# First tile of the input projection from the unnormed input, and the memory's keys and values beside the input's norm

## What is computed

```python
def rms_norm(x, g, eps=EPS):
    return x * lax.rsqrt(jnp.mean(x * x, axis=-1, keepdims=True) + eps) * g

def reference(x, mem, ...):
    mkv = (rms_norm(mem, mem_norm_g) @ mem_w_kv).reshape(B, M, 2, MEM_HEADS, MEM_HEAD_DIM)
    mem_k = rms_norm(mkv[:, :, 0], mem_k_g)
    mem_v = mkv[:, :, 1]
    for l in range(DEPTH):
        h = rms_norm(x, norm_mix_g[l])
        proj = h @ w_in[l]
        ...
```

## Time and profile before

| | us |
|---|---|
| median of 3 runs | 2043.94 |
| lowest, highest | 2038.11, 2048.75 |
| profiled execution | 2036.31 |
| its span, first to last instruction | 2034.5 |
| TensorE matmuls, busy | 1954.1 (96% of the span) |
| VectorE busy | 637.1 |
| ScalarE busy | 385.8 |
| GpSimd busy | 74.4 |
| granted TensorE clock, mean | 0.994 |

### The profile page before, as it was taken

One profiled execution on the slowest core, in us unless ns is written; L12 is line 12 of the kernel. 1 busy time (PEld: TensorE's weight loads), 2 busy tenths in 40 slices (PEclk: granted clock), 3 DMA queues, 4 the chain that ended last, 5 costly groups with the idle time before them and its releaser, 6 DMA issues. The chain is left out here.

```text
span 2034.5 us, 27414 instructions
## 1 busy us (share of the span) xinstructions
PE 1954.1 (96%) x11538; PEld 1049.1 (52%) x11538; DVE 637.1 (31%) x1297; ACT 385.8 (19%) x739; POOL 74.4 (4%) x138
## 2 busy tenths in 40 slices
PE   8999999999999999999799999989999999999996
PEld 5445995455544444443254489754554444444443
DVE  4244665224311111111144556551452111111112
ACT  3221325224000000000122222350520000000001
POOL 3000000000000000000200010010000000000001
PEclk9999999999999999999999999999999999999998
DMA  8000001521699999999850000032239999999996
GB/s 351 1 1 0 3 3 50 207 83 42 261 410 426 427 427 429 428 429 427 333 214 1 0 2 3 10 139 110 83 124 393 423 428 427 429 429 428 427 428 237
DMA packets 51548, 481.88 MB, mean 237 GB/s; under 512 B 7216, under 2 KB 12080, under 8 KB 23792
## 3 DMA queue, kind: packets, MB, share of 16 engines
q1 hardware_dynamic: 49136, 471.91, 55.7%
q0 software_dynamic: 2304, 8.39, 1.1%
HBM read 461.14 MB, written 19.14 MB: 236 GB/s over the span
## 5 line engine op out<-in xcount | busy, mean ns | idle before, releaser
L1898 PE MATMUL bank<-ring,hT 128*64 128x512 f32 x2080 | 471.3, 596 | 14.0 <-DVE hT L1928 8.3
L1898 PEld LDWEIGHTS bank<-ring,hT 128*64 128x64 f32 x2080 | 143.2, 137 | 286.9 <-issue 264.2
L842 PE MATMUL bank<-hT,ring 128*128 128x512 f32 (+1 forms) x608 | 263.3, 594 | 1.8 <-DVE hT L289 1.0
L1891 PE MATMUL bank<-arena 128*128 128x256 f32 x1088 | 252.0, 386 | 3.8 <-DVE arena L1918 3.8
L1891 PEld LDWEIGHTS bank<-arena 128*128 128x128 f32 x1088 | 201.9, 190 | 78.9 <-issue 50.3
L1905 PE MATMUL bank<-ring,arena 128*64 128x512 f32 x1040 | 236.7, 597 | 5.5 <-DMA ring<-in_we 4.5
L842 PEld LDWEIGHTS bank<-hT,ring 128*128 128x128 f32 (+1 forms) x608 | 114.3, 189 | 148.0 <-issue 146.9
L1928 DVE TENSOR_TENSOR hT<-bank,colp 128x512 f32<-128x512 f32 x68 | 47.0, 692 | 399.6 <-PE bank L1891 399.6
L2188 ACT ACTIVATE arena<-bank 128x256 f32<-128x256 f32 x65 | 24.9, 383 | 662.3 <-PE bank L1877 662.3
L1905 PEld LDWEIGHTS bank<-ring,arena 128*64 128x64 f32 x1040 | 70.6, 137 | 143.7 <-issue 136.3
L2338 DVE COPY arena<-bank 128x512 f32<-128x512 f32 x65 | 45.0, 692 | 257.1 <-PE bank L1905 257.1
(11 more groups left out here) (435 smaller groups left out, 1988.4 us busy)
## 6 DMA issues: line engine op xcount, KB each, us to landing
ring<-in_we SPq DMA_DIRECT2D x195, 2048.0 KB, 17.6
expert_rows<-arena SPq DMA_DIRECT2D x130, 128.0 KB, 15.0
ring<-in_w_in SPq DMA_DIRECT2D x6, 2048.0 KB, 19.5
ring<-in_w_out SPq DMA_DIRECT2D x4, 2048.0 KB, 9.6
ring<-in_wm SPq DMA_DIRECT2D x2, 2048.0 KB, 7.8
ring<-in_w_in SPq DMA_DIRECT2D x2, 1920.0 KB, 17.0
ring<-in_w_in SPq DMA_DIRECT2D x2, 1664.0 KB, 28.1
ring<-in_w_in SPq DMA_DIRECT2D x2, 1152.0 KB, 30.7
```

What stands on the lines that cost most here:

```text
L842: last = nc.tensor.matmul(B[n % 4][0:w, :], ins_units[unit][:, k, u0:u0 + w], hT[:, k, :], start=k == 0, stop=k == KD - 1)
L1891: last = nc.tensor.matmul(bank[:, o:o + GS], htok[:, i, k * P:(k + 1) * P], selg[z][:, i, :], start=i == 0, stop=i == NT - 1)
L1898: last = nc.tensor.matmul(bank[CAP * j:CAP * j + CAP, :], x[:, k, :], up_w(u, j, k), start=k == 0, stop=k == KD - 1)
```

## The change

The projection is linear, and the norm multiplies each token by one factor, so that factor can stand behind the product. The change uses this for the first of the 19 tiles in both layers: GpSimd multiplies the gain into the 128 columns of unit 3 that the tile uses (`scale_first`), TensorE multiplies them with `xT` itself, and VectorE applies `rsx` when it copies the tile out of PSUM (this took ScalarE's `evict(0)`). The norm's last mean is put between the second and the third product of that tile. From tile 1 on, `hT` is used as before.

In the setup the same is done for the memory: `memh` is now mem times gain only. The keys are multiplied by the memory's factors when copied from PSUM (`scale_keys`), the values by a per-token column (`m_tok`) in ScalarE's copy. The squares of the memory are summed over k by one VectorE reduction (`msum`), those of x by four (`sum_tokens`), each with a step between the elements it adds, so TensorE needs one product for each mean. Layer 0's roots, reciprocals and `hT` move from the setup behind the barrier. `memcol` and `wkv` move up in the queue of transfers, the columns behind unit 3. Scratch moves into `hT`, which is free then. The filler products ahead of the keys (L512) and ahead of layer 1's projection go away.

```diff
+        def scale_first(eng, lay):
+            eng.wait_ge(s_win[3], 16 * lay + 16)
+            eng.wait_ge(s_col, 16 * lay + 16)
+            w = ins_units[3][:, :, 0:P]
+            eng.tensor_tensor(w, w, colp[:, COLS["g_mix"]:COLS["g_mix"] + KD].unsqueeze(2).to_broadcast([P, KD, P]),
+                              ALU.mult).then_inc(s_w1, 1)
...
                 eng.dma_start(memx, memT_d).then_inc(s_im, 16)
+                eng.dma_start(memcol, memcol_d).then_inc(s_mc, 16)
+                eng.dma_start(wkv, wkv_d).then_inc(s_ik, 16)
                 eng.dma_start(smalli[:, 0:NT], pos_d).then_inc(s_in, 16)
                 eng.dma_start(small[:, 0:HALF], inv_d).then_inc(s_in, 16)
-                eng.dma_start(memcol, memcol_d).then_inc(s_in, 16)
                 eng.dma_start(xT[:, :, :], xT_d).then_inc(s_ix, 16)
+                load_w_in(eng, slice(0, 1), (3,))
                 load_columns(eng, slice(0, 1))
-                eng.dma_start(wkv, wkv_d).then_inc(s_ik, 16)
-                load_w_in(eng, slice(0, 1), (3, 1, 0, 2, 4, 5))
+                load_w_in(eng, slice(0, 1), (1, 0, 2, 4, 5))
...
             @block.vector
-                eng.wait_ge(s_in, 16 * 3)
+                eng.wait_ge(s_mc, 16)
+                eng.wait_ge(s_im, 16)
+                for k in range(KD):
+                    eng.tensor_scalar(memh[:, k, :], memx[:, k, :], memcol[:, k:k + 1], None,
+                                      ALU.mult).then_inc(s_mh, 1)
+                eng.wait_ge(s_msq, 2)
+                eng.tensor_reduce(msum, msq.rearrange("p k t -> p t k"), AX, ALU.add).then_inc(s_msm, 1)
+                eng.wait_ge(s_in, 16 * 2)
...
-                eng.wait_ge(s_mrt, 1)
...
-                token_scale(eng, "g_mix")
+                eng.wait_ge(s_mrt, 2)
+                v(eng.reciprocal(m_rs, m_rs))
+                eng.reciprocal(m_tok, m_tok).then_inc(s_mrr, 1)
+
+                def sum_tokens(i):
+                    eng.wait_ge(s_xsq, i + 1)
+                    eng.tensor_reduce(xsum[:, i * P:(i + 1) * P], sqx[i % 2].rearrange("p k t -> p t k"), AX,
+                                      ALU.add).then_inc(s_xsm, 1)
+
+                def scale_keys(c):
+                    eng.wait_ge(s_mkv, c + 1)
+                    eng.tensor_tensor(kraw[:, c, :], B[4 + c][:, 0:MEM], m_rs, ALU.mult).then_inc(s_mkr, 1)
+                scale_keys(0)
+                sum_tokens(0)
+                scale_keys(1)
+                for i in range(1, NT):
+                    sum_tokens(i)
...
             @block.scalar
+                eng.activation(small[:, 628:629], epsc[:, 0:1], ACT.Sqrt)
...
+                for z in range(2):
+                    eng.activation(msq[:, 4 * z:4 * z + 4, :], memx[:, 4 * z:4 * z + 4, :],
+                                   ACT.Square).then_inc(s_msq, 1)
+                eng.wait_ge(s_mms, 1)
+                eng.activation(m_rs, B[0][:, 0:MEM], ACT.Sqrt, bias=epsc[:, 0:1]).then_inc(s_mrt, 1)
+                eng.activation(m_tok, B[1][:, 0:2], ACT.Sqrt, bias=epsc[:, 0:1]).then_inc(s_mrt, 1)
                 eng.wait_ge(s_done, 1)
...
+                eng.activation(small[:, 628:629], epsc[:, 0:1], ACT.Sqrt)
...
+                for i in range(NT):
+                    square_tokens(i)
...
             @block.tensor
...
-                eng.wait_ge(s_mh, KD)
-                eng.wait_ge(s_rt, NT)
...
+                eng.wait_ge(s_msm, 1)
+                nc.tensor.matmul(B[0][:, 0:MEM], ones_mean[:, :], msum, start=True, stop=True)
+                for i in range(2):
+                    last = nc.tensor.matmul(B[1][:, i:i + 1], msum[:, i * P:(i + 1) * P], ones_mean[:, 0:1],
+                                            start=True, stop=True)
+                last.then_inc(s_mms, 1)
+                eng.wait_ge(s_ik, 16)
+                keys(0)
+                keys(1)
+                values(0)
+                values(1)
...
@@ layer, gpsimd
                         combine_gather(eng, ys_d[0:NE * CAP, :])
+                        scale_first(eng, layer)
...
@@ layer, scalar
+                        eng.wait_ge(s_x0, 1)
+                        for i in range(NT):
+                            eng.activation(rsx[:, i * P:(i + 1) * P], B[3][:, i * P:(i + 1) * P], ACT.Sqrt,
+                                           bias=epsc[:, 0:1]).then_inc(s_rt, 1)
-                    evict(0)
+                    eng.wait_ge(s_pad, 1)
                     evict(1)
...
@@ layer, vector
-                    if layer:
-                        for i in range(NT):
-                            token_factors(eng, i)
-                        token_scale(eng, "g_mix")
-                    else:
+                    for i in range(NT):
+                        token_factors(eng, i)
+                    token_scale(eng, "g_mix")
+                    eng.wait_ge(s_pj, 1)
+                    eng.tensor_tensor(shp[:, 0, 1:SEQ + 1], B[0][:, :], rsx, ALU.mult).then_inc(s_pad, 1)
+                    if not layer:
...
@@ layer, tensor
-                        for i in range(1, NT):
+                        for i in range(1, NT - 1):
                             token_means(eng, i, B[2 * i], s_xsq, s_xms)
-                        keep_busy(B[1], 6, P)
+
+                    def first_products(k0, k1):
+                        for k in range(k0, k1):
+                            last = nc.tensor.matmul(B[0][:, :], ins_units[3][:, k, 0:P], xT[:, k, :], start=k == 0,
+                                                    stop=k == KD - 1)
+                        return last
+                    eng.wait_ge(s_w1, layer + 1)
...
+                    first_products(0, 2)
+                    if layer:
+                        token_means(eng, NT - 1, B[2 * NT - 2], s_xsq, s_xms)
+                    else:
+                        nc.tensor.matmul(B[3][:, :], ones_mean[:, :], xsum, start=True, stop=True).then_inc(s_x0, 1)
+                    first_products(2, KD).then_inc(s_pj, 1)
...
+                    for n, j in list(enumerate(TILE_ORDER))[1:]:
```

More of the change, by code:

```diff
@@ L330, in combine_adds @@
             combine_add(eng, NT - 1)
+        spare = hT[:, :, :].rearrange("p k t -> p (k t)")
+        xsum = spare[:, 3584:4096]
         s_in = sem("inputs_loaded")
@@ L350, in build @@
         wkv = arena[:, 4096:8192].rearrange("p (k n) -> p k n", k=KD)
-        msq = ring_view(5, 2048, 512).rearrange("p (c t) -> p c t", c=2)
+        msq = spare[:, 0:2048].rearrange("p (k t) -> p k t", k=KD)
+        msum = spare[:, 2048:2048 + MEM]
+        kraw = arena[:, 0:512].rearrange("p (c t) -> p c t", c=2)
+        m_rs, m_tok = small[:, 256:512], small[:, 512:514]
         ksq = ring_view(5, 2560, 512).rearrange("p (c t) -> p c t", c=2)
@@ L461, in _ @@
                 eng.sem_inc(s_done, 1)
-                eng.wait_ge(s_mrt, 1)
-                rs = small[:, 256:512]
-                v(eng.reciprocal(rs, rs))
-                for k in range(KD):
-                    eng.scalar_tensor_tensor(out=memh[:, k, :], in0=memx[:, k, :], scalar=memcol[:, k:k + 1],
-                                             in1=rs, op0=ALU.mult, op1=ALU.mult).then_inc(s_mh, 1)
-                eng.wait_ge(s_col, 16)
-                for i in range(NT):
-                    token_factors(eng, i)
-                token_scale(eng, "g_mix")
+                eng.wait_ge(s_mrt, 2)
[13 more added lines that the diff above has]
+                    sum_tokens(i)
             @block.scalar
@@ L520, in _, with values @@
                     last.then_inc(s_mkv, 1)
-                for i in range(2):
+                def values(i):
                     for k in range(KD):
@@ L721, in _ @@
                             v(eng.reciprocal(krs[:, c, :], krs[:, c, :]))
-                            eng.scalar_tensor_tensor(out=memKT[:, c, :], in0=B[4 + c][:, 0:MEM], scalar=memcol[:, 8:9],
+                            eng.scalar_tensor_tensor(out=memKT[:, c, :], in0=kraw[:, c, :], scalar=memcol[:, 8:9],
                                                      in1=krs[:, c, :], op0=ALU.mult, op1=ALU.mult).then_inc(s_kd, 1)
```

60 lines of the change are left out of this document (27 added, 33 removed).

## The result

| | before | after |
|---|---|---|
| median, lowest to highest, us | 2043.94 (2038.11 to 2048.75) | 2032.48 (2027.11 to 2034.05) |
| ratio, 95% interval | | 0.9945 [0.9923, 0.9967] |
| executions | 5 | 5 |
| profiled execution; its span | 2036.31; 2034.5 | 2032.48; 2030.7 |

The profiled executions differ by only 3.8 us, where the forecast had 10.4 from the trace. So the gain is nearer 0.4% than 0.55%, and the forecast's time was met by luck: two errors cancel. This is what the experiments had to sort out.

The account below looks back on a forecast made before the run. It took the last wait before the projection's second tile as the bound, in setup and layer 1. Gains of 8.2 (setup with layer 0) and 2.2 (layer 1) made 10.4 us: 2043.94 to 2033.5, range 2029 to 2038.5.

Parts of the forecast that it names:

- The base: Whole kernel: the median of before, 2043.94 us, from which the gain of 10.4 was subtracted.
- Start and multiplies: Setup: VectorE starts at 6.0 and makes eight 128x256 multiplies at 0.35 us each, 2.8 us, to 8.8.
- The lock on the port: Setup: GpSimd's fills could delay each of VectorE's eight multiplies by 0.22 us, making the gain 1.8 us smaller.
- The reduction: Setup: VectorE's sum of 2048 elements over k takes 2.3 us, to 11.1; bound above 4.6 us.
- Rival 1: Setup: the stepped reduction costs twice, keys 2.3 us later, gain 8.1, time 2035.8; chance 0.20.
- Slow first matmuls: Setup: TensorE at half pace until 14.6; mean and columns end at 13.3, keys and values lose 0.65 us.
- Rival 3: Setup: TensorE's clock stays low through all 64 passes of keys and values, 13.2 us more, time 2046.7; chance 0.04.
- Barrier, tile 0, `hT`: Setup's end and layer 0: last matmuls 1.03 us, barrier 0.81; tile 0's mean gives back 0.86; hT margin 0.25.
- rival 2: Layer 0: roots and reciprocals run strictly in sequence, tile 1 waits 0.9 us, gain 9.3, time 2034.6; chance 0.12.
- Layer 1: Head of layer 1: tile 1 starts 2.4 us sooner with the mean between tile 0's products; 2.2 taken.
- May hold one up by 0.5 us: Head of layer 1: GpSimd's weight scaling beside VectorE's merges may delay one merge by 0.5 us.
- The upper end: Whole kernel: a gain of 12.5 us with columns, clock and multiplies at their lower ends.

Follow-up runs that it names:

- near_squares: The changed kernel with layer 1's weight multiply on ScalarE, and ScalarE writing each token's eight squares side by side; 2028.59 us, ratio 0.9946 to before.
- warm_setup: The changed kernel with layer 1's weight multiply on ScalarE, plus 28 filler products on TensorE in the setup; 2026.81 us, ratio 0.9926 to before.
- pool_late: The changed kernel with GpSimd's weight multiply in layer 1 moved behind its fills; 2029.65 us, ratio 0.9951 to before.
- after_again: The changed kernel measured once more, unchanged; 2033.17 us, ratio 0.9969 to before.

## Why the prediction was right in the time and not in the sum

**The base.** The forecast subtracted from a median that was 5 us too high (2043.94 against 2039). The gain was too large by 2.4 to 4.6 us (10.4 against 5.8 and 7.7 by medians). The two cancel in 2033.5, which is luck. The spread of before had been given as 3 us for a median; the profiled execution, 7.6 below, was the hint, and I read it only as an offset.

**Start and multiplies: right.** 5.98 for 6.0, and 2.58 us for 2.8. The lock on the port, weighed there at 1.8 us, did not show: with GpSimd's fills beside them the eight took 0.32 us each, less than the 0.35 taken.

**The reduction: mis-sized, 3.60 for 2.3.** It ended at 12.1 instead of 11.1. Rival 1 came true in kind, at 1.57 times and not twice; the rule of the Trainium skill that stood beside it (SBUF — State Buffer, section "Door 1: The DMA port swizzle") agrees in sign. "No row shows a penalty for a step" was no evidence against one: no row had the step. `near_squares` gives the 2.29 without it. Of the 2.3 us that rival 1 asks for, 1.3 came.

**Slow first matmuls: mis-sized.** From the reduction's end to the keys it took 1.85 us (2.2 forecast). Keys and values took 16.1 for 14.5, since the half pace lasted until 18 and not 14.6: 2.3 us lost for 0.65. I had taken its length from one place behind an idle stretch; here the keys alone took 9.36, 9.20 and 8.25 us in three executions of one kernel. `warm_setup` shows that it hangs on what TensorE did before and not on the products. Rival 3, in which it lasts through all 64 passes, had the right mechanism but six times the loss: 13.8 us against 2.3.

**Barrier, tile 0, `hT`: right.** The last two matmuls and the barrier took 1.70 for 1.84; tile 0 with its mean 7.80 for 7.7; no wait at tile 1 (rival 2 fell). `hT`'s first multiply ended 0.3 us ahead of need, for 0.25. So the setup and tile 0 gained 6.0, 6.1 and 7.1 us (45.5 less 39.53, 39.48 and 38.42) in three executions, for 8.2.

**Layer 1: the step that failed.** Forecast 2.2 us gained, measured 0.8 to 1.5 lost in the heads. The idea itself was sized rightly: from the end of mean 2 to tile 1 it took 8.5 us (8.65 forecast), and with the multiply on ScalarE the heads are 31.0, 30.4, 30.9, 30.7 and 30.6, which is 2.3 below the 33.0 of the three heads before. "May hold one up by 0.5 us", for which the 2.2 leaves 0.2, is what failed: the multiply held a merge up by 1.8 to 2.1 us. In all four executions TensorE's clock then fell (0.69, 0.84, 0.69 and 0.69 over 11 us), for another 1 to 2 us; that the wait for the merge brought this about fits, but the waits of `pool_late` and `after_again` do not show it. The same lock had been named in the prediction, for a place where it did not show.

**The parts and the whole.** Setup and tile 0 less the loss in layer 1 make 4.6, 5.3 and 5.8 us in the three executions. The medians say 5.8 and 7.7, each good to some 4. The parts account for the gain within that, and no closer.

**Sums.** Rival 2 takes 0.9 off 10.4, which is 9.5 and not 9.3. The upper end, with columns 0.95, clock 0.65 and the start of the reduction 0.9 sooner (ScalarE's squares end at 7.9), is 12.9 and not 12.5. Neither matters to what came.

**Rest.** The two columns of work that no edit touched show no saved time coming back in the experts, but they spread by 4 and 6 us, so a return of 1 or 2 us would not be seen.

The chances were 0.49 for a gain over 0.5% and 0.48 for less. One comparison of three lies over that line, the first, and its base was high; the other two put the gain at 0.3 and 0.4%. So "less" deserved more than half.

## What to carry to other kernels

Price a GpSimd operation that may meet a VectorE operation with two SBUF inputs on the critical path at its full duration, and place it beside work that reads PSUM, or give it to an engine that waits there anyway. When a layout puts a step between neighbours (here 1 KB in reads, 32 bytes in writes), ask both the writer and the reader what it costs; moving it from one to the other can be a zero sum. When a dense stretch on TensorE follows idleness, its first products can run at half pace: 28 filler products in the idle time ahead gave 2.2 us back. And compare against a base of many runs before judging a sum of 0.5%.

## What the runs showed of the hardware

- A merge of 1.28 us took 3.12 to 3.40 us beside a 1.9 us multiply of GpSimd, in four executions of four, and ended 1.08 to 1.10 us behind the multiply's end in five of five. A GpSimd fill of 0.67 us took 1.45 and 1.58 us beside a merge of VectorE. Two adds with one input in PSUM kept their 1.27 us.
- A reduction of 2048 float32 took 3.60 us with 1 KB between the elements it adds, 2.29 with none; of 1024, 1.91 (512 B) and 1.22. A 128x1024 square on ScalarE took 1.05 us writing in line and 2.08 writing with a step of 32 B.
- TensorE ran at half pace for 4 us of continuous products in the setup while the granted clock read 1.00; 8.85 us of fillers ahead removed it.
- Of one kernel, executions with a mean granted clock of 0.986 and 0.994 differed by 15 us; the time fell about 2 us for each 0.001.
